# Two wide adding transfers of the input in place of four, in a two-layer hybrid decoder trunk

## What is computed

```
for l in range(DEPTH):
    mod = (cond @ w_ada[l] + b_ada[l])[:, None, :]
    sh1, sc1, g1, sh2, sc2, g2 = jnp.split(mod, 6, axis=-1)
    h = rmsnorm(x, norm_g[l, 0]) * (1.0 + sc1) + sh1
    proj = h @ w_in[l]
    ...
    x = x + g1 * (jnp.concatenate([a_out, o_out], axis=-1) @ w_out[l])
    h2 = rmsnorm(x, norm_g[l, 1]) * (1.0 + sc2) + sh2
    gate, up = jnp.split(h2 @ w_gate_up[l], 2, axis=-1)
    x = x + g2 * ((jax.nn.silu(gate) * up) @ w_down[l])
```

## The kernel before

| tile | sums by VectorE | POOL, in order |
|---|---|---|
| 40 | 134 (1), 135 (2) | adding transfer 0, loads 140 (1), 141 (2) |
| 41 | 136 (12), 137 (14), 138 (0) | load 142 (0) |
| 42 | 139 (7), 140 (1) | adding transfer 1, loads 143 (7), 144 (1) |
| 43 | 141 (2), 142 (0), 143 (7) | loads 145 (3), 146 (4), 147 (5), 151 (2), 149 (0), 148 (7) |
| 44 | 144 (1) | adding transfer 2, load 150 (1) |
| 45 | 145 (3), 146 (4) | loads 152 (6), 153 (8), 154 (3), 155 (4) |
| 46 | none | adding transfer 3 |
| 47 | 147 (5), 148 (7) | loads 156 (5), 157 (7) |
| 49 | 149 (0), 150 (1) | loads 158 (0), 159 (1) |

## Time and profile before

### The profile page before, as it was taken

The page is one execution under the profiler, slowest core; times in us unless marked ns, Lnnn a source line. Parts: engine busy times, 40 slices in busy tenths (PEclk is TensorE's granted clock), DMA queues, the critical chain, the costliest instruction groups (busy, mean ns, idle before and its releaser), DMA issues.

```text
span 2176.5 us, 25306 instructions
## 1 busy us (share of the span) xinstructions
PE 2128.0 (98%) x9624; PEld 1686.5 (77%) x9624; DVE 1552.2 (71%) x2276; ACT 985.3 (45%) x1521; POOL 209.1 (10%) x392
## 2 busy tenths in 40 slices
PE   7899999999999999999999999999999999999999
PEld 3345778788888888888878778878888888888887
DVE  6767999797687888788777774678765555555545
ACT  2123664744344434343465475574443443444443
POOL 3212112011011111111101100001100000000000
PEclk9899999999999999999999999999999999999999
DMA  9999899799588888888857865458855555555554
GB/s 391 412 390 400 319 367 356 276 354 349 194 331 333 315 328 305 318 322 325 304 190 265 318 246 189 159 193 320 300 211 193 191 194 193 188 182 193 192 193 155
DMA packets 112028, 595.97 MB, mean 274 GB/s; under 512 B 12642, under 2 KB 13090, under 8 KB 65188
## 3 DMA queue, kind: packets, MB, share of 16 engines
q1 hardware_dynamic: 55232, 390.83, 48.3%
q0 software_dynamic: 56384, 203.45, 25.1%
q10 hardware_dynamic: 292, 0.09, 0.0%
HBM read 592.18 MB, written 2.13 MB: 273 GB/s over the span
## 4 chain that ended last, share of the span: by engine, by line
PE 86%; DVE 5%; DMA 4%; issue 2%; ACT 2%; ACTq 0%; DVEq 0%
PE ps L641 75%; PE ps L701 2%; DVE w_lo L1603 1%; DMA ada<-w_ada 1%; DMA raw<-stream 1%; DVE ada L1633 1%; DMA kT<-w_ada 1%; PE ps L1070 1%; PE ps L965 1%; PE ps L934 1%; DMA qT<-w_ada 1%; PE ps L1011 1%; ACT w_hi L1188 1%; PE ps L613 1%; PE ps L618 1%
## 5 line engine op out<-in xcount | busy, mean ns | idle before, releaser
L1603 DVE TENSOR_TENSOR w_lo<-raw,w_hi 128x1024 fp32r<-128x1024 f32 x664 | 798.4, 1222 | 342.0 <-ACT w_hi L1188 341.6
L1188 ACT ACTIVATE w_hi<-raw 128x1024 fp32r<-128x1024 f32 x664 | 693.2, 1057 | 631.4 <-PE ps L641 596.0
L641 PE MATMUL ps<-w_hi,h_hi 128*128 128x512 f32 x1696 | 466.4, 397 | 1.4 <-DVE h_lo L1716 1.4
L641 PE MATMUL ps<-w_hi,h_lo 128*128 128x512 f32 x1696 | 454.4, 390 | 0.0
L641 PE MATMUL ps<-w_lo,h_hi 128*128 128x512 f32 x1696 | 454.0, 389 | 0.0
L641 PEld LDWEIGHTS ps<-w_hi,h_lo 128*128 128x128 f32 x1696 | 318.3, 188 | 67.6
L641 PEld LDWEIGHTS ps<-w_lo,h_hi 128*128 128x128 f32 x1696 | 318.3, 188 | 67.3
L641 PEld LDWEIGHTS ps<-w_hi,h_hi 128*128 128x128 f32 x1696 | 313.3, 188 | 67.8 <-issue 4.2
L641 PE MATMUL ps<-w_hi,a_hi 128*128 128x512 f32 x848 | 234.4, 398 | 0.0
L641 PE MATMUL ps<-w_hi,a_lo 128*128 128x512 f32 x848 | 227.0, 389 | 0.0
L641 PE MATMUL ps<-w_lo,a_hi 128*128 128x512 f32 x848 | 226.9, 389 | 0.0
(11 more groups left out here) (230 smaller groups left out, 1604.2 us busy)
## 6 DMA issues: line engine op xcount, KB each, us to landing
raw<-stream SPq DMA_DIRECT2D x360, 1024.0 KB, 5.0
ada<-w_ada POOLq DMA_DIRECT2D x180, 512.0 KB, 6.8
qT<-w_ada POOLq DMA_DIRECT2D x52, 512.0 KB, 7.2
uc<-w_ada POOLq DMA_DIRECT2D x29, 512.0 KB, 7.7
gate<-w_ada POOLq DMA_DIRECT2D x27, 512.0 KB, 11.1
kT<-w_ada POOLq DMA_DIRECT2D x26, 512.0 KB, 8.0
val<-w_ada POOLq DMA_DIRECT2D x25, 512.0 KB, 7.9
pT<-w_ada POOLq DMA_DIRECT2D x25, 512.0 KB, 6.7
```

The costliest lines, as they stand in the source:

```text
L641: mm = pe.matmul(banks[tok][0][:], x_part[:, tok * P:(tok + 1) * P], w[:, k, :], start=first and a == 0 and i == 0 and k == 0, stop=last a ...
L1188: act.activation(whi[h % 4][:].rearrange("p k c -> p (k c)"), raw[t % 4][:, a * 1024:(a + 1) * 1024], ACT.Copy).then_inc(hi_ready.sem, 1)
L1603: dve.tensor_tensor(wlo[h % 4][:].rearrange("p k c -> p (k c)"), raw[t % 4][:, a * 1024:(a + 1) * 1024], whi[h % 4][:].rearrange("p k c -> ...
```

## The change

The four adding transfers become two, each of 1024 columns of both token blocks (1 MB). The first is issued at tile 42 and waits for the first two updates, the second at tile 46 and waits for all four. There are two semaphores in place of four, and each add of the second pass waits for that of its half.

```diff
-X_AT = (40, 42, 44, 46)
+X_AT = (42, 46)
...
-        x_added, turned_landed = [count(f"x_added{n}") for n in range(4)], count("turned_landed")
+        x_added, turned_landed = [count(f"x_added{n}") for n in range(2)], count("turned_landed")
...
                     if layer == 0 and t in X_AT:
                         n = X_AT.index(t)
-                        cols = slice(n * 512, (n + 1) * 512)
-
-                        pool.wait_ge(x_updated.sem, x_updated.at(here, 2 * n + 2))
+                        cols = slice(n * ADA_K, (n + 1) * ADA_K)
+
+                        pool.wait_ge(x_updated.sem, x_updated.at(here, 4 * n + 4))
                         pool.dma_start(x[:, :, cols], x_in.rearrange("(q p) d -> p q d", p=P)[:, :, cols],
                                        accum_op=ALU.add).then_inc(x_added[n].sem, 16)
...
                 if place.layer == 0 and c < C_MLP:
-                    dve.wait_ge(x_added[3].sem, 16)
+                    dve.wait_ge(x_added[1].sem, 16)
...
                     if here.layer == 0 and 4 <= m < 8:
-                        dve.wait_ge(x_added[n].sem, 16)
+                        dve.wait_ge(x_added[n // 2].sem, 16)
```

## The result

The changed kernel takes 2186.9 us (median of 22 runs, 2180.97 to 2194.81), the kernel before 2183.05 us in the runs beside them (22 runs). The ratio is 1.0019, with a 95% interval of 1.0011 to 1.0028: 2.4 to 6.1 us slower, less than the 0.3% set as the bound for a change. The forecast was 2.3 us slower, 2184.5 us, within 2179.5 to 2190.0. Of the 2.4 us between 2184.5 and 2186.9, 0.8 us are the kernel before, whose median was 2182.21 us in three runs and is 2183.05 in 22. The profiled execution has a span of 2179.6 us against 2176.5.

What follows compares the result with a forecast made beforehand. The prediction took VectorE, not TensorE, to bound the touched stretch. A 2.3 us stall for uc, all other terms 0, added to the 2182.21 us median gave 2184.5 us, range 2179.5 to 2190.0.

Steps and rivals of the forecast that it cites:

- The bound in the stretch: About 342 to 380 us: VectorE works end to end, so a microsecond lost there is one of the total.
- Item 1: Transfers at tiles 40 and 44 gone: POOL's saved issue time and earlier loads behind them worth 0.
- Item 2: Joined transfer at tile 42 delays uc's load by 2.5 us; less 0.2 us slack, VectorE stands 2.3 us.
- the idle 0.42 us: Time the DMA engines stood idle in 332 to 338 us, which the longer transfer was to fill.
- the 2.96 us of engine time: Cost on the DMA engines of 512 KB more of adding, taken as proportional to bytes.
- Item 3: After the uc stall: TensorE, with 3.3 us slack after h_lo, stops only at the norm, by 2.3 us.
- Item 4: Joined transfer at tile 46 lands at 378.3, wanted at 379.56 plus the 2.3 us delay; costs 0 us.
- Rival A: Joined transfer holds POOL's queue no longer than a single one, uc is in time; 2182.2 us, chance 0.30.
- Rival B: Long adding rows dearer than in proportion, uc late at 342.02; at 12 us, stall 8.4, time 2190.6; chance 0.10.
- C: Faster by more than 6.5 us, from an emptier queue; chance 0.03.
- D: Join undone below, rows cut into 2 KB pieces as before; same 2.3 us, only queue 0's packets tell; chance 0.05.

Runs made afterwards that it cites:

- the plain copy: Changed kernel with its first joined transfer copying instead of adding, so part of layer 0's first update is lost; ratio 0.9991 to the kernel before, no wait.
- pairs: Four single transfers of 512 columns, issued two at a time at the changed kernel's tiles 42 and 46; ratio 1.0014 to the kernel before.
- first pair joined alone: Kernel before with only its first two transfers joined, at tile 42, the other two single at tiles 44 and 46; ratio 1.0017.
- changed, again: The changed kernel run a second time, nothing altered; 2188.52 against 2182.09 us for the kernel before, ratio 1.0036.
- changed, a third time: The changed kernel run once more, nothing altered, for the scatter of its wait; ratio 1.0016 to the kernel before.
- pairs, again: Second run of the four single transfers issued two at a time at tiles 42 and 46; ratio 1.0031 to the kernel before.
- the loads-first order: Changed kernel with each tile's loads issued ahead of its adding transfer; ratio 1.0046 to the kernel before. The same order in the kernel before: 1.0023.

## Why the prediction was right, and where it was off

- **The bound in the stretch** (VectorE's work end to end, from uc to the norm): right. The chain runs the same way after the change, with the load of uc put into it, and 4.7 us of delay at 346.75 are still 4.76 us at 389.78 and 4.74 us near 1000 us. One reading was incomplete: VectorE has two pauses of 1.75 us for ScalarE's w_hi before the change, at 360.21 and at 371.40, not one. Both are there after it, at the same length, so neither absorbs anything, as was argued for the one.
- **Item 1, two transfers gone:** worth 0, as forecast; all four gone are worth 0 too.
- **Item 2, uc behind the joined transfer:** right in place and mechanism, and the plain copy shows that the adding makes it. Its size was the term that was off: uc was to land 2.5 us later after its issue, and in the three profiles of the changed kernel it landed 3.0, 4.4 and 4.7 us later. Neither part of the 2.5 is shown wrong by itself: nearly all of the idle 0.42 us was filled, and the 2.96 us of engine time lie between the two workings above. What failed is the step from a mean time of 16 engines to a landing, taken from one execution as if it had no scatter. The kernel before and all six profiles with 1 MB of adding ahead of uc (us after issue; for the pairs, after the first one's):

  | profile | adding transfer landed | uc landed | wait for uc |
  |---|---|---|---|
  | before (512 KB of adding) | 7.4 | 5.3 | none |
  | pairs | 12.5 | 8.1 | 2.5 |
  | changed | 12.4 | 8.3 | 2.8 |
  | first pair joined alone | 12.4 | 8.8 | 3.2 |
  | changed, again | 12.8 | 9.7 | 4.2 |
  | changed, a third time | 13.1 | 10.0 | 4.4 |
  | pairs, again | 13.2 | 10.6 | 5.1 |

  The wait is what uc's landing takes beyond 5.5 us, to 0.1 us in each of them. The mean of the changed kernel's three is 3.8 us, beside the 3.9 us measured, so the forecast was low by about 1.5 us; its 2.3 us lie just below the measured 2.4 to 6.1. Why the landing differs between executions is not settled, but it is not the order of issues: in all six, uc is issued 6.2 or 6.3 us after the adding transfer, and the loads of the weight stream 2.4 or 2.5 and 9.4 or 9.5 us after it.
- **Item 3, what hangs on it:** the slack of 3.3 us at h_lo was right to a tenth of a us, as the pauses of 0.84, 1.09 and 1.8 us show. That TensorE loses it only at the norm was wrong in place: it stopped 2.6 us in the last pair of tiles before the norm. The sum is about the same as the wait (2.8 us).
- **Item 4, the second joined transfer:** no wait, as forecast. It landed at 382.3, about 2 us later than the forecast's 378.3 plus the 1.9 us of this execution, and left 2.0 us of 3.5.
- **Rival A** (no wait) falls by six profiles with 1 MB of adding at tile 42. The Trainium skill, DMA: Bandwidth & Descriptors, section Anatomy of one DMA, gives about 2.0 us fixed per transfer. No such time was saved by joining here: a pair of single transfers took 12.5 and 13.2 us to the last landing, a joined one 12.4 to 13.1. **Rival B** (4 KB rows far dearer) falls by the same comparison. **C** falls by the kernel without the transfers, **D** by the packet count.

## What to carry to other kernels

Joining transfers in one in-order queue is a matter of what stands behind them, not of their number: look for the load with the least slack behind the new place, and put the wide transfer where nothing wanted soon follows (one tile earlier cost nothing here). An adding transfer counted here as more than twice its bytes (2.96 against 1.27 us of the engines for 512 KB). When the slack is 0.2 us, read the landing in several executions and not in one: here it varied by 2.5 us. And to find what a change costs, compare the same instruction in both traces just ahead of its place and well behind it; that told the wait to 0.1 us, where the medians varied by several.

## What the runs showed of the hardware that I had not expected

The first adding transfer of 1 MB, at tile 41 or 42, took 12.4 to 13.2 us from issue to landing, the plain copy of the same rows at the same place 6.1 us. POOL's issue followed the rows and the kind, not the bytes: 1.26 us for 1 MB and 1.25 us for 512 KB when adding, 0.71 us for the plain 1 MB. And the loads-first order turned a wait for uc into one for x 45 us later: its DMA share was 0.69 in 333.2 to 339.2 us and 0.71 in 339.2 to 345.2, where the changed kernel, 1.2 us ahead of it, has 0.83 and 1.02 in 332 to 338 and 338 to 344, and its last transfer landed 30 us after issue in place of 23. That fits a queue that never gets back the time in which it was left idle; no run isolated it.
